# Rotary queries and keys projected channels-first, with partner channels fetched by transfers within SBUF

## The chip, the cores and the metric

One core of one Trainium2 chip runs the whole program in one launch. The metric is the device time in microseconds. Its median over three runs of the kernel before is 974.03 us (973.75 to 974.24).

## What is computed

A decoder trunk of two layers over 256 tokens of 1024 channels, float32. Each layer is a SwiGLU block, a hybrid mixer and a second SwiGLU block, each followed by a layer norm. The change touches the mixer alone, and in it the eight rotary heads (group C):

```python
def rope(t, positions):                      # HEAD_DIM = 64
    ang = positions[:, None] * inv[None, :]  # 32 frequencies
    ang = concatenate([ang, ang], axis=-1)
    t1, t2 = split(t, 2, axis=-1)
    return t * cos(ang) + concatenate([-t2, t1], axis=-1) * sin(ang)

def hybrid_mixer(x, ...):
    proj = x @ w_in
    a_val, a_gate, bq, bk, bv, bf, cq, ck, cv = split(proj, ...)
    y_a = conv_module(a_val, a_gate, ...)            # 256 channels, causal, 31 taps
    y_b = forgetting_attention(bq, bk, bv, bf, ...)  # 4 heads of 64, no rotary
    qc = rope(heads(cq, 8), positions) * (64 ** -0.5)
    kc = rope(heads(ck, 8), positions)
    y_c = dilated_attention(qc, kc, cv)              # 8 heads of 64
    return concatenate([y_a, y_b, y_c]) @ w_o
```

Queries and keys are 512 columns each of `x @ w_in`. The partner of channel c of a head is channel c + 32 or c - 32 of the same head.

## The kernel before

All work is ordered by hand: five engine programs (SyncE, TensorE, ScalarE, VectorE, GpSimd), each run in its written order, tied by counting semaphores. TensorE is called PE, ScalarE ACT, VectorE DVE below, as in the profile.

Weights arrive in units of 128 x 2048 values (1 MB) in a ring of three slots. For each unit ACT rounds the raw values to `w_hi` (`split_hi`, L888), DVE forms the rest `w_lo` (`split_lo`, L1113), and PE uses three products per piece, hi x hi, hi x lo and lo x hi. A slot's next `split_hi` waits until PE has used the slot (`unit_used`), and its next load until `split_lo` is done (`lo_done`). The mixer's units are 0 and 1 (convolution input), 2 and 3 (rotary queries), 4 and 5 (rotary keys), 6 (values and forget gates of group B), 7 and 8 (values of group C), 9 and 10 (queries and keys of group B), 11 to 14 (output projection).

Two forms of projection exist. `project` (L463 to L481) holds 128 tokens of the input as PE's stationary operand and streams 512 weight columns past it: 12 matmuls of 512 columns for a unit and a tile of tokens, 24 for a unit; the result has tokens on the partitions. `project_T` (L741 to L756) holds 128 weight columns and streams the 256 tokens: 48 matmuls of 256 columns for a unit; the result has channels on the partitions. Before the change only units 9 and 10 use `project_T`.

The order of the mixer around the change (`mixer` of each engine: PE L802, ACT L995, DVE L1361):

- PE: units 2 and 3 into `ybank[0:2]`, with the transposes of the convolution's input (`conv_input_T`) between them; units 4 and 5 into `ybank[2:4]`; `rotated_T` for n = 0, 1 (four 128 x 128 transposes each, through L426); unit 6 into `bank[0:2]`; unit 7; `rotated_T` for n = 2, 3; unit 8; then eight steps of attention. A step takes the scores of a pair of heads (L670), the transposes of the previous pair's probabilities (`probs_T`, L426), the products with the values of that pair (`values`, L737), and between these the pieces of units 9 to 14 that `FILL` lists.
- DVE: `split_lo` of units 5 to 10, and between them the rotation `rope(l, n)` (L1251 to L1270; n = 0, 1 queries and n = 2, 3 keys of token tile n % 2), which reads the projection in PSUM, twice multiplies and once adds 128 x 512 values; `gate_sums` behind `split_lo(8)`; `log_gates` behind `split_lo(9)`; and the 31 taps of the convolution (`taps`, L1283, two instructions a tap) in the gaps: 5 taps after `gate_sums`, 4 after `log_gates`, the last in step 5. In a step DVE masks the scores and takes their maximum (`mask_and_max`, L1338), and normalises the probabilities (`inverse`, `normalise`).
- ACT: `split_hi` of units 5 to 10, and between them `rotated_out(n)` (L1014 to L1019), which copies the transposed queries and keys out of PSUM into `qT` and `kT`, the values' copies (L1027, L1041) and the gates' exponential and logarithm. In a step it copies the transposed probabilities of the previous pair's first head (`probs_out`, L1044), takes the exponentials of this pair's two heads (`exponent`, L1050), and only then copies those of the previous pair's second head.
- PE's waits in the steps that matter here: `values` waits for both heads' transposed probabilities (L724), the transposes of the convolution's result (`conv_out_T`, L697 to L703) for the last tap.

Of the kernel before, what the change touches and what calls it, by code (L numbers as in the profile page):

```python
# [20 lines left out]
ALU = mybir.AluOpType  # L21
# [3 lines left out]
P = 128  # L25
SEQ, D, DEPTH = 256, 1024, 2
T = SEQ // P
KT = D // P
# [77 lines left out]
def consts_array():  # L106
# [4 lines left out]
    cos = np.cos(ang).astype(np.float32).reshape(T, P, 32).transpose(1, 0, 2).reshape(P, -1)  # L111
    sin = np.sin(ang).astype(np.float32)
    sgn = np.concatenate([-sin, sin], axis=1).reshape(T, P, 64).transpose(1, 0, 2).reshape(P, -1)
# [15 lines left out]
def trunk(nc, x, w_in, w_o, ffn_in, ffn_out, ln_gb, conv_wb, rows, consts, out):  # L129
    with ExitStack() as ctx:  # L130
        def sb(name, shape, dt=F32):
            return ctx.enter_context(nc.sbuf_tensor(name, shape, dt))
# [35 lines left out]
        rope_c = sb("rope_c", [P, DIL_H * HD])  # L168
        rope_s = sb("rope_s", [P, DIL_H * HD])
        qk = sb("qk", [P, 2, DIL_H * HD])  # L170
# [21 lines left out]
        for width in (P, 2 * P, 2 * CAUSAL, T * 32, T * 64):  # L192
# [3 lines left out]
        cos_t = cos_t.rearrange("p (t e) -> p t e", t=T)  # L196
        sin_t = sin_t.rearrange("p (t e) -> p t e", t=T)
# [44 lines left out]
        rope_mul = counted("rope_mul", 2 * T)  # L242
        rope_ready = counted("rope_ready", 2 * T)
# [12 lines left out]
        qk_psum = counted("qk_psum", 2 * T)  # L256
        qkT_ready = counted("qkT_ready", 2 * T + 2)
# [155 lines left out]
        def _(eng):  # L413
# [236 lines left out]
            def scores(l, s):  # L650
# [13 lines left out]
                eng.wait_ge(qkT_ready, count(qkT_ready, l, 2 * T + 2 * fox))  # L664
# [22 lines left out]
            def gate_sums_T(l):  # L687


                eng.wait_ge(lf_ready, count(lf_ready, l, 2))  # L690
                eng.wait_ge(qkT_ready, count(qkT_ready, l, 2 * T))
# [20 lines left out]
            def probs_T(l, p, i):  # L712

                h = 2 * p + i
                eng.wait_ge(p_ready, count(p_ready, l, h + 1))
                if h > 0:

                    eng.wait_ge(pT_ready, count(pT_ready, l, h))
                transposes(bank[2], [prob[:, h % 4, j * P:(j + 1) * P] for j in range(3)]).then_inc(pT_psum, 1)
# [21 lines left out]
            def project_T(slot, half, m, last_unit=None):  # L741
# [4 lines left out]
                dst, cols = ybank[m // 2][:, (m % 2) * SEQ:(m % 2 + 1) * SEQ], slice(m * P, (m + 1) * P)  # L746
# [43 lines left out]
            def rotated_T(l, which, last_unit):  # L790

                for n in which:

                    eng.wait_ge(rope_ready, count(rope_ready, l, n + 1))
                    if n == 1:
                        eng.wait_ge(uT_ready, count(uT_ready, l, 1))
                    if n >= 2:
                        eng.wait_ge(qkT_ready, count(qkT_ready, l, n - 1))
                    transposes(bank[3 - n % T], [qk[:, n % T, p * P:(p + 1) * P] for p in range(4)],
                               last_unit if n % T == 0 else None).then_inc(qk_psum, 1)  # L800

            def mixer(l):  # L802
# [15 lines left out]
                def halves(u, dst, last_unit=None, between=None, at=None):  # L818

                    for half in range(2):  # L820
                        wait_unit(l, b + u + half)
                        for t in range(T):
                            m = project(dst[t][:, :], (u + half) % RING, half, t,
                                        last_unit=last_unit if half == t == 0 else None)
# [4 lines left out]
                            if half == 0 and t == at:  # L829
                                between()  # L830
# [6 lines left out]
                halves(2, ybank[0:2], unit_used, conv_input_T, 0)  # L837
                halves(4, ybank[2:4], unit_used)
                rotated_T(l, range(2), unit_used)

                wait_unit(l, b + 6)
                for t in range(T):
                    project(bank[t][:, 0:FVF], 6 % RING, 0, t, FVF, KT).then_inc(proj_done, 1)
# [36 lines left out]
        def _(eng):  # L880
# [26 lines left out]
            def begin_sum(l, j, t):  # L907

                if j == 1 and t == 0:
                    eng.wait_ge(qkT_ready, count(qkT_ready, l, 2 * T + 2))  # L910
# [84 lines left out]
            def mixer(l):  # L995
# [4 lines left out]
                for t in range(T):  # L1000
# [13 lines left out]
                def rotated_out(n):  # L1014
                    t = n % T
                    eng.wait_ge(qk_psum, count(qk_psum, l, n + 1))
                    dst = (qT, kT)[n // T]
                    eng.activation(dst[:, :, t * P:(t + 1) * P], bank[3 - t][:, :].rearrange("p (k n) -> p k n", k=4),
                                   ACT.Copy, scale=-HD ** -0.5 if n < T else 1.0).then_inc(qkT_ready, 1)  # L1019

                rotated_out(0)
                rotated_out(1)
# [11 lines left out]
                rotated_out(2)  # L1034
                rotated_out(3)
# [18 lines left out]
                for s in range(STEPS):  # L1054
# [13 lines left out]
                    for i in range(2 if s == FQ_STEP else 0):  # L1068
# [3 lines left out]
                                       ACT.Copy, scale=(-HD ** -0.5, 1.0)[i]).then_inc(qkT_ready, 1)  # L1072
# [33 lines left out]
        def _(eng):  # L1106
# [144 lines left out]
            def rope(l, n):  # L1251

                t, src = n % T, ybank[n]
                eng.wait_ge(proj_done, count(proj_done, l, T + n + 1))
                if n > 0:

                    eng.wait_ge(rope_ready, count(rope_ready, l, n))
                eng.tensor_tensor(rope_c[:, :].rearrange("p (g e) -> p g e", e=32),
                                  src[:, :].rearrange("p (g e) -> p g e", e=32),
                                  cos_t[:, t:t + 1, :].broadcast_to([P, 2 * DIL_H, 32]), ALU.mult)  # L1260
                halves = dict(h=DIL_H, s=2)
                swapped = src[:, :].rearrange("p (h s e) -> p h s e", **halves)[:, :, ::-1, :]
                sin4 = sin_t[:, t, :].rearrange("p (h s e) -> p h s e", h=1, s=2).broadcast_to([P, DIL_H, 2, 32])
                eng.tensor_tensor(rope_s[:, :].rearrange("p (h s e) -> p h s e", **halves), swapped, sin4, ALU.mult)\
                   .then_inc(rope_mul, 1)
                if n >= T:

                    eng.wait_ge(qk_psum, count(qk_psum, l, n - T + 1))
                eng.wait_ge(rope_mul, count(rope_mul, l, n + 1))
                eng.tensor_tensor(qk[:, n % T, :], rope_c[:, :], rope_s[:, :], ALU.add).then_inc(rope_ready, 1)  # L1270
# [90 lines left out]
            def mixer(l):  # L1361
# [139 lines left out]
```

## Time and profile before

| | |
|---|---|
| median of three runs | 974.03 us |
| the profiled execution | 973.58 us |
| its span, first to last instruction | 971.8 us |
| PE, DVE, ACT busy | 959.7, 654.5, 503.1 us |
| mixer of layer 0, from its first projection to the second block's | about 201 to 308 us of the span |
| mixer of layer 1 | about 680 to 787 us |

The profile is one execution on the chip. A timeline gives for each instruction its start and its length; neighbours on one engine overlap a little in it, since an instruction's tail is counted in its length, so the pace of a queue is read from the starts. An entry in brackets is the idle time ahead of an instruction and what ended it. The chain of work that ended last is followed back from the last instruction. The two mixers run alike, 478.57 us apart, so the first stands for both.

### The profile page before, as it was taken

What the parts mean: (1) busy time and instruction counts of PE and PEld (TensorE: products, weight loads), DVE (VectorE), ACT (ScalarE), POOL (GpSimd) and SP (SyncE); (2) the same over time, 40 slices, a digit from 0 to 9 for tenths busy, and PEclk for the clock granted to TensorE, in tenths of its full rate; (3) what the DMA queues carried; (4) which work ended last, traced back from release to release, by engine and by line L of the source; (5) the groups of instructions that cost most, each with busy time, mean ns of one, the idle gap of its engine ahead of it and who ended that gap; (6) DMA issues with size and microseconds to landing.
All of it is one profiled execution on the core that took longest, in us unless ns stands there. A gap on an engine that the chain in (4) does not pass through costs nothing.

```text
span 971.8 us, 14695 instructions
## 1 busy us (share of the span) xinstructions
PE 959.7 (99%) x5263; PEld 814.8 (84%) x5263; DVE 654.5 (67%) x950; ACT 503.1 (52%) x672; POOL 29.1 (3%) x27
## 2 busy tenths in 40 slices
PE   8999999999999999999999999999999999999997
PEld 6988888888878988888888888888888788888885
DVE  6555656689998565655675565657999875565565
ACT  6454455445774445545454455544457654554541
POOL 0000000010001000000010000002000010000000
PEclk9999999999999999999999999999999999999999
DMA  9656566565325656557555656565643355655551
GB/s 313 235 173 216 173 202 227 188 217 174 131 88 162 228 173 200 188 182 245 166 186 174 215 174 196 193 219 183 233 162 115 120 194 175 194 195 176 197 189 43
DMA packets 123586, 180.05 MB, mean 185 GB/s; under 512 B 5792, under 2 KB 98080, under 8 KB 122784
## 3 DMA queue, kind: packets, MB, share of 16 engines
q1 hardware_dynamic: 123264, 178.91, 55.6%
q0 software_dynamic: 144, 0.62, 0.2%
q8 instruction: 22, 0.36, 0.1%
q14 instruction: 12, 0.10, 0.0%
q10 hardware_dynamic: 144, 0.07, 0.0%
HBM read 178.52 MB, written 1.05 MB: 185 GB/s over the span
## 4 chain that ended last, share of the span: by engine, by line
PE 98%; DVE 1%; ACT 0%; issue 0%; DVEq 0%
PE bank L549 27%; PE bank L551 14%; PE ybank L500 10%; PE ybank L506 10%; PE ybank L504 10%; PE bank L426 3%; PE bank L472 2%; PE bank L479 2%; PE bank L476 2%; PE ybank L472 2%; PE ybank L479 2%; PE ybank L476 2%; PE bank L533 2%; PE bank L529 2%; PE bank L535 2%; PE bank L670 1%
## 5 line engine op out<-in xcount | busy, mean ns | idle before, releaser
L1113 DVE TENSOR_TENSOR w_lo<-raw,w_hi 128x2048 fp32r<-128x2048 f32 (+1 forms) x155 | 355.2, 2292 | 241.5 <-ACT w_hi L888 241.5
L888 ACT ACTIVATE w_hi<-raw 128x2048 fp32r<-128x2048 f32 x160 | 305.8, 1911 | 254.7 <-PE ybank L506 112.8
L549 PE MATMUL bank<-xT,w_hi 128*128 128x512 f32 x1152 | 401.0, 392 | 0.0
L551 PE MATMUL bank<-xT,w_lo 128*128 128x256 f32 x1152 | 323.7, 281 | 0.0
L549 PEld LDWEIGHTS bank<-xT,w_hi 128*128 128x128 f32 x1152 | 216.3, 188 | 47.3
L551 PEld LDWEIGHTS bank<-xT,w_lo 128*128 128x128 f32 x1152 | 216.7, 188 | 1.5
L500 PE MATMUL ybank<-w_hi,yT_hi 128*128 128x512 f32 x416 | 165.9, 399 | 0.3
L506 PE MATMUL ybank<-w_hi,yT_lo 128*128 128x512 f32 x416 | 162.9, 392 | 0.0
L504 PE MATMUL ybank<-w_lo,yT_hi 128*128 128x512 f32 x416 | 161.9, 389 | 0.0
L500 PEld LDWEIGHTS ybank<-w_hi,yT_hi 128*128 128x128 f32 x416 | 78.2, 188 | 18.0 <-issue 2.6
L506 PEld LDWEIGHTS ybank<-w_hi,yT_lo 128*128 128x128 f32 x416 | 77.8, 187 | 18.4
L504 PEld LDWEIGHTS ybank<-w_lo,yT_hi 128*128 128x128 f32 x416 | 78.2, 188 | 14.4
L937 ACT ACTIVATE gate<-gate 128x256 f32<-128x256 f32 x72 | 30.1, 418 | 48.4 <-DVE gate L1194 48.4
L930 ACT ACTIVATE gate<-bank 128x256 f32<-128x256 f32 x72 | 27.7, 385 | 51.1 <-PE bank L551 51.1
L1283 DVE SCALAR_TENSOR_TENSOR acc<-uT,cwb,acc 128x256 f32<-128x256 f32 x120 | 50.2, 479 | 0.1
L472 PE MATMUL bank<-w_hi,xT 128*128 128x512 f32 (+1 forms) x112 | 41.5, 370 | 1.3 <-ACT xT L903 1.3
L1194 DVE TENSOR_TENSOR gate<-bank,gate 128x256 f32<-128x256 f32 x72 | 30.3, 421 | 16.8 <-ACT gate L930 16.8
L476 PE MATMUL bank<-w_lo,xT 128*128 128x512 f32 (+1 forms) x112 | 40.4, 361 | 0.0
L1201 DVE TENSOR_TENSOR hid<-gate,hid 128x256 f32<-128x256 f32 x72 | 30.6, 426 | 11.5 <-ACT gate L937 11.5
L472 PE MATMUL ybank<-w_hi,xT 128*128 128x512 f32 x96 | 38.2, 398 | 0.0
L479 PE MATMUL ybank<-w_hi,xT 128*128 128x512 f32 x96 | 37.7, 393 | 0.0
L476 PE MATMUL ybank<-w_lo,xT 128*128 128x512 f32 x96 | 37.6, 392 | 0.0
(133 smaller groups left out, 986.6 us busy)
## 6 DMA issues: line engine op xcount, KB each, us to landing
raw<-in_ffn_in SPq DMA_DIRECT2D x172, 512.0 KB, 4.6
raw<-in_ffn_out SPq DMA_DIRECT2D x88, 512.0 KB, 3.9
raw<-in_w_in SPq DMA_DIRECT2D x40, 512.0 KB, 4.5
raw<-in_w_o SPq DMA_DIRECT2D x16, 512.0 KB, 3.6
gb<-in_ln_gb SPq DMA_DIRECT2D x6, 1024.0 KB, 7.2
raw<-in_w_in SPq DMA_DIRECT2D x4, 520.0 KB, 6.2
raw<-in_ffn_in SPq DMA_DIRECT2D x8, 256.0 KB, 5.4
xn<-in_x SPq DMA_DIRECT2D x4, 256.0 KB, 4.3
```

Source lines behind the costliest of these rows:

```text
L472: m = eng.matmul(dst, xT_hi[:, kk, tok], wh[:, k, :], start=kk == 0 and not onto, stop=False, skip_group_check=onto)
L476: m = eng.matmul(dst, xT_hi[:, kk, tok], wl[:, k, :], start=False, stop=False, skip_group_check=onto)
L479: m = eng.matmul(dst, xT_lo[:, kk, tok], wh[:, k, :], start=False, stop=kk == KT - 1, skip_group_check=onto)
L500: m = eng.matmul(dst, aT_hi[:, k, tok], wh[:, k, cols], start=False, stop=False, skip_group_check=True)
L504: eng.matmul(dst, aT_hi[:, k, tok], wl[:, k, cols], start=False, stop=False, skip_group_check=True)
L506: m = eng.matmul(dst, aT_lo[:, k, tok], wh[:, k, cols], start=False, stop=ends is not None and k == 1, skip_group_check=True)
L549: eng.matmul(dst[:, :], wh[:, k, g, cols], xT[:, kk, :, :].rearrange("p a n -> p (a n)"), start=kk == 0, stop=False, skip_group_check=True)
L551: m = eng.matmul(dst[:, SEQ:2 * SEQ], wl[:, k, g, cols], xT_hi[:, kk, :], start=False, stop=kk == KT - 1, skip_group_check=True)
L888: eng.activation(w_hi[:, s, 0:width], raw[:, s, 0:width], ACT.Copy).then_inc(hi_done, 1)
L1113: eng.tensor_tensor(w_lo[:, s, 0:width], raw[:, s, 0:width], w_hi[:, s, 0:width].bitcast(F32), ALU.subtract).then_inc(lo_done, 1)
L1201: eng.tensor_tensor(hid[:, j, :], gate[:, j, :], hid[:, j, :], ALU.mult).then_inc(h_ready, 1)
L1283: eng.scalar_tensor_tensor(acc[:, cb, :], src, w, acc[:, cb, :], ALU.mult, ALU.add)\
```

## The change

Units 2 to 5 are projected by `project_T`, so the queries and keys leave PE with channels on the partitions, two heads to a bank half. ACT copies them from PSUM to `qk_raw` (two copies of 128 x 512 for the queries, two for the keys) and scales the queries there. Four transfers of 32 partitions x 4 KB each, issued from ACT's queue behind the copies, write every 32-channel half to the place of its partner in `qk_swap`. DVE multiplies `qk_raw` by the cosines into `qT` or `kT` (`rope_cos`), multiplies `qk_swap` by the signed sines once the transfers have landed, and adds (`rope_sin`); each is one instruction of 128 x 1024 values. PE's sixteen transposes a layer (`rotated_T`) and ACT's four copies behind them (`rotated_out`) are gone. The tables of cosines and sines grow from 192 to 512 columns of the constants.

```diff
@@ PE
+                def halves_T(u, first_bank, between=None):
+                    for half in range(2):
+                        wait_unit(l, b + u + half)
+                        for m in range(4):
+                            e = project_T((u + half) % RING, half, m, unit_used if half == m == 0 else None, first_bank)
+                            if half == 1 and m % 2 == 1:
+                                e.then_inc(proj_done, 1)
...
-                halves(2, ybank[0:2], unit_used, conv_input_T, 0)
-                halves(4, ybank[2:4], unit_used)
-                rotated_T(l, range(2), unit_used)
+                halves_T(2, 0, conv_input_T)
+                halves_T(4, 2)
...
-                eng.wait_ge(rope_mul, count(rope_mul, l, 2 * T))
-                halves(7, ybank[2:4], unit_used, lambda: rotated_T(l, range(2, 4), None), 1)
+                eng.wait_ge(qk_copied, count(qk_copied, l, 4))
+                halves(7, ybank[2:4])
@@ ACT
+                def rotary_out(n):
+                    for i in range(2):
+                        eng.wait_ge(proj_done, count(proj_done, l, T * (n + 1) + i + 1))
+                        eng.activation(qk_raw[:, n, 2 * i:2 * i + 2, :],
+                                       ybank[2 * n + i][:, :].rearrange("p (k n) -> p k n", k=2), ACT.Copy,
+                                       scale=(-HD ** -0.5, 1.0)[n]).then_inc(qk_copied, 1)
+                    eng.wait_ge(qk_copied, count(qk_copied, l, 2 * n + 2))
+                    for g in range(4):
+                        to, of = 32 * g, 32 * (g + 1 - 2 * (g % 2))
+                        eng.dma_start(qk_swap[to:to + 32, n, :, :], qk_raw[of:of + 32, n, :, :])\
+                           .then_inc(swap_loaded[n], 16)
                 split_hi(l, b, 5)
+                rotary_out(0)
                 split_hi(l, b, 6)
                 split_hi(l, b, 7)
...
-                rotated_out(0)
-                rotated_out(1)
+                rotary_out(1)
                 split_hi(l, b, 8)
...
-                rotated_out(2)
-                rotated_out(3)
                 split_hi(l, b, 10)
@@ DVE
+            def rope_cos(l, n):
+                eng.wait_ge(qk_copied, count(qk_copied, l, 2 * n + 2))
+                eng.tensor_tensor((qT, kT)[n][:, :, :], qk_raw[:, n, :, :],
+                                  cos_t.broadcast_to([P, DIL_H // 2, SEQ]), ALU.mult).then_inc(rope_mul, 1)
+            def rope_sin(l, n):
+                eng.wait_ge(swap_loaded[n], count(swap_loaded[n], l, 64))
+                eng.tensor_tensor(qk_swap[:, n, :, :], qk_swap[:, n, :, :],
+                                  sin_t.broadcast_to([P, DIL_H // 2, SEQ]), ALU.mult).then_inc(rope_mul, 1)
+                eng.wait_ge(rope_mul, count(rope_mul, l, 2 * n + 2))
+                eng.tensor_tensor((qT, kT)[n][:, :, :], (qT, kT)[n][:, :, :], qk_swap[:, n, :, :], ALU.add)\
+                   .then_inc(rope_ready, 1)
...
                 split_lo(l, b, 5)
-                rope(l, 0)
+                rope_cos(l, 0)
                 split_lo(l, b, 6)
-                rope(l, 1)
                 taps(l, TAPS_AT["unit", 6])
                 split_lo(l, b, 7)
-                rope(l, 2)
-                rope(l, 3)
+                rope_sin(l, 0)
+                rope_cos(l, 1)
                 split_lo(l, b, 8)
                 gate_sums(l)
+                rope_sin(l, 1)
                 taps(l, TAPS_AT["unit", 8])
                 split_lo(l, b, 9)
```

The semaphores follow: the scores wait for `rope_ready` where they waited for `qkT_ready`, `project_T` takes the number of its first bank, and the release of unit 5's slot moves to the first matmul of unit 6.

## Rows read from the trace of the kernel before

**Rows 1.** The page's busy times and the chain that ended last.

```profile
PE 959.7 (99%) x5263; PEld 814.8 (84%) x5263; DVE 654.5 (67%) x950; ACT 503.1 (52%) x672; POOL 29.1 (3%) x27
PE 98%; DVE 1%; ACT 0%; issue 0%; DVEq 0%
```

**Rows 2.** Chain that ended last, layer 0 (start us, length us, what): the removed transposes.

```profile
229.54 0.87 PE bank L426 x8
...
241.68 0.87 PE bank L426 x8
```

**Rows 3.** Timeline of PE, 512 columns (start, length, engine, line, operation, operands, count).

```profile
210.21 0.39 PE L476 MATMUL ybank<-w_lo,xT 128*128 128x512 f32 x1
...
229.15 0.39 PE L479 MATMUL ybank<-w_hi,xT 128*128 128x512 f32 x1
```

**Rows 4.** Timeline of PE, 256 columns, piece (9, 0, 1) to (9, 1, 1).

```profile
251.24 0.28 PE L753 MATMUL ybank<-xT,w_hi 128*128 128x256 f32 x1
...
255.29 0.28 PE L754 MATMUL ybank<-xT,w_lo 128*128 128x256 f32 x1
```

**Rows 5.** Timeline of ACT around units 7 to 9.

```profile
224.05 1.92 ACT L888 ACTIVATE w_hi<-raw 128x2048 fp32r<-128x2048 f32 x1 [3.31 <-PE ybank L479]
230.02 1.09 ACT L1018 ACTIVATE qT<-bank 128x512 f32<-128x512 f32 x2 [4.05 <-PE bank L426]
230.99 1.92 ACT L888 ACTIVATE w_hi<-raw 128x2048 fp32r<-128x2048 f32 x1
...
236.21 0.39 ACT L1027 ACTIVATE fv<-bank 128x256 f32<-128x256 f32 x1 [2.49 <-PE bank L479]
```

**Rows 6.** Timeline of DVE from unit 8's `split_lo` to step 1's mask.

```profile
233.70 2.28 DVE L1113 TENSOR_TENSOR w_lo<-raw,w_hi 128x2048 fp32r<-128x2048 f32 x1
235.90 0.15 DVE L1313 TENSOR_TENSOR fz<-bank,small 128x4 f32<-128x4 f32 x1
236.63 0.16 DVE L1313 TENSOR_TENSOR fz<-bank,small 128x4 f32<-128x4 f32 x1 [0.57 <-ACT fv L1027]
...
236.91 4.04 DVE L1283 SCALAR_TENSOR_TENSOR acc<-uT,cwb,acc 128x256 f32<-128x256 f32 x10
...
249.03 0.29 DVE L1338 CUSTOM_DVE_ANT_0 masked<-bank,cst 128x128 f32<-128x128 f32 x1 [0.35 <-PE bank L670]
...
256.45 0.29 DVE L1338 CUSTOM_DVE_ANT_0 masked<-bank,cst 128x128 f32<-128x128 f32 x1 [0.97 <-PE bank L670]
...
257.01 0.08 DVE L1338 DVE_READ_ACCUMULATOR2_ANT negmax<- 128x1 f32 x1
```

**Rows 7.** DVE groups by shape: count, then busy us and mean ns of one.

```profile
L1144 DVE TENSOR_TENSOR w_lo<-raw,w_hi 128x1024 fp32r<-128x1024 f32 x5 | 6.1, 1219 | 0.0
L1270 DVE TENSOR_TENSOR qk<-rope_c,rope_s 128x512 f32<-128x512 f32 x8 | 5.5, 693 | 0.6
```

**Rows 8.** DMA issues: ACT's only one, in its timeline; then SP's of L358 (ns min/median/max) and their landing.

```profile
0.75 0.41 ACTq L1096 DMA_DIRECT2D cst<-in_consts  x1
...
L358 SPq DMA_DIRECT2D raw<-in_w_in x44: 367/418/615, 171.3 to 708.7; - x44
...
DMA to landing us min/median/max: 3.1/4.1/6.8
```

**Rows 9.** Timeline of all engines in step 1: exponential, second copy, products with the values.

```profile
257.32 0.39 ACT L1050 ACTIVATE prob<-masked,negmax 128x128 f32<-128x128 f32 x1
...
259.08 0.48 ACT L1044 ACTIVATE probT<-bank 128x384 f32<-128x384 f32 x1
...
260.00 0.63 PEld L737 LDWEIGHTS bank<-probT,cv 128*64 128x64 f32 x8
```

**Rows 10.** Timeline of all engines where the convolution's last tap meets PE.

```profile
284.49 0.87 DVE L1283 SCALAR_TENSOR_TENSOR acc<-uT,cwb,acc 128x256 f32<-128x256 f32 x2
...
284.89 0.49 PE L426 MATMUL bank<-cst,prob 128*128 128x128 f32 x3
...
285.51 0.63 PE L426 MATMUL bank<-cst,acc 128*128 128x128 f32 x4
```

More of the change, by code:

```diff
@@ L191, in trunk @@
         at, view = 0, []
-        for width in (P, 2 * P, 2 * CAUSAL, T * 32, T * 64):
+        for width in (P, 2 * P, 2 * CAUSAL, SEQ, SEQ):
             view.append(cst[:, at:at + width])
@@ L241, in trunk @@
         u_ready = counted("u_ready", T)
-        rope_mul = counted("rope_mul", 2 * T)
-        rope_ready = counted("rope_ready", 2 * T)
+        qk_copied = counted("qk_copied", 4)
+        swap_loaded = [counted(f"swap_loaded{n}", 4 * 16) for n in range(2)]
+        rope_mul = counted("rope_mul", 4)
+        rope_ready = counted("rope_ready", 2)
         cv_ready = counted("cv_ready", T)
@@ L662, in scores @@
                 qs, ks = (fqT, fkT) if fox else (qT, kT)
-                eng.wait_ge(qkT_ready, count(qkT_ready, l, 2 * T + 2 * fox))
+                if fox:
+                    eng.wait_ge(fqkT_ready, count(fqkT_ready, l, 2))
+                else:
+                    eng.wait_ge(rope_ready, count(rope_ready, l, 2))
                 for t, (cols, keys) in enumerate(((slice(0, P), P), (slice(P, CAUSAL), SEQ))):
@@ L718, in probs_T @@
                     eng.wait_ge(pT_ready, count(pT_ready, l, h))
+                else:
+                    eng.wait_ge(uT_ready, count(uT_ready, l, 1))
                 transposes(bank[2], [prob[:, h % 4, j * P:(j + 1) * P] for j in range(3)]).then_inc(pT_psum, 1)
@@ L739, in values, with project_T @@
                 m.then_inc(pv_done, 1)
-            def project_T(slot, half, m, last_unit=None):
+            def project_T(slot, half, m, last_unit=None, first_bank=0):
                 wh = w_hi[:, slot, 0:UNIT].rearrange("p (k n) -> p k n", k=4)
                 wl = w_lo[:, slot, 0:UNIT].rearrange("p (k n) -> p k n", k=4)
-                dst, cols = ybank[m // 2][:, (m % 2) * SEQ:(m % 2 + 1) * SEQ], slice(m * P, (m + 1) * P)
+                dst = ybank[first_bank + m // 2][:, (m % 2) * SEQ:(m % 2 + 1) * SEQ]
+                cols = slice(m * P, (m + 1) * P)
                 for k in range(4):
@@ L788, in fill @@
                         m.then_inc(unit_used, 1)
[L790 to L800, printed above, removed]
             def mixer(l):
@@ L816, in mixer, with halves @@
                     project(bank[t][:, :], 1, 1, t).then_inc(proj_done, 1)
-                def halves(u, dst, last_unit=None, between=None, at=None):
+                def halves(u, dst):
                     for half in range(2):
@@ L823, in halves @@
                             m = project(dst[t][:, :], (u + half) % RING, half, t,
-                                        last_unit=last_unit if half == t == 0 else None)
+                                        last_unit=unit_used if half == t == 0 else None)
                             if half == 1:
@@ L828, in halves @@
                                 m.then_inc(unit_used, 1)
-                            if half == 0 and t == at:
+                def halves_T(u, first_bank, between=None):
[5 more added lines that the diff above has]
+                                e.then_inc(proj_done, 1)
+                            if half == 0 and m == 3:
+                                e.then_inc(unit_used, 1)
+                            if half == 0 and m == 1 and between is not None:
                                 between()
@@ L909, in begin_sum @@
                 if j == 1 and t == 0:
[L910 removed]
+                    eng.wait_ge(fqkT_ready, count(fqkT_ready, l, 2))
                 elif j == 1:
```

47 lines of the change are left out of this document (11 added, 36 removed).

## The prediction, made before the changed kernel was run

> **What bounds the kernel now.** I read the page first: PE is busy 99% of the span and makes 98% of the chain that ended last [rows 1]. So a microsecond of PE work removed is worth a microsecond, unless PE then meets a wait that its own work covers today. Both mixers must therefore be read queue by queue, to see how far behind PE the other two engines are where PE waits for them. Two places matter. In step 1 PE loads the first values' weights at 260.00, while the copy that it needs begins at 259.08 and ends at 259.56 [rows 9]: ACT is 0.44 us ahead of PE, no more. At the end of the convolution DVE's last tap ends at 284.49 + 0.87 = 285.36, PE's preceding transposes end at 285.38, and the transposes of the taps' result follow at 285.51 [rows 10]: DVE and PE arrive together. A faster PE alone gains nothing beyond these two meetings. The question is what the change does to DVE and ACT.
>
> **PE: what goes and what comes.** Two blocks of eight transposes leave the chain, 0.87 us each [rows 2], 1.74 us a layer. In their place 96 matmuls of 512 columns become 192 of 256. The columns streamed are the same; the pace is not. From the start at 210.21 to that at 229.15 lie 82 matmuls of 512: 0.2310 us each [rows 3]. From 251.24 to 255.29 lie 34 of 256: 0.1191 us each [rows 4]. So 192 x 0.1191 - 96 x 0.2310 = 22.87 - 22.18 = 0.69 us more. PE alone would be 1.74 - 0.69 = 1.05 us a layer ahead at the end of unit 8, 2.1 us in all. These prices come from this trace in the same form and the same bank pattern, so I give them 0.1 us a layer of doubt.
>
> **ACT: four copies stay four copies, eight issues are new.** Of the copies only the place changes: the old ones read 128 x 512 from PSUM as the new ones do. New is that ACT issues four transfers behind each pair. The only issue of ACT in the trace takes 0.41 us; SP's take 0.37 to 0.62, median 0.42 [rows 8]. I take 0.42, so 1.68 us for four; the bounds are 0 (the queue hands them over and goes on) and 0.62. The first four push units 6's `split_hi` from 218.8 to about 221.2 and its `split_lo` to about 225.4; PE wants unit 6 at about 230.1, so this is covered. The second four are not covered. PE ends unit 5 at 229.38 + 0.69 = 230.07, with its tail 230.25. ACT's last copy ends at 230.85, the issues at 232.6, and `split_hi(8)` runs from 232.6 to 234.5, where it began at 230.99 [rows 5]. PE itself wants unit 8 only at about 241.4, so the wait behind is DVE's.
>
> **DVE: the same work, placed later.** Twelve instructions of 128 x 512 (0.69 us) become six of 128 x 1024, 1.22 us by the row of that shape [rows 7]. That is 8.3 against 7.3 us, a small gain, but in the wrong place: before, all four rotations are done when `split_lo(8)` begins at 233.70. After, that `split_lo` waits for ACT until 234.5, ends its slot at 236.7, the two small sums and the minimum follow to about 237.05, and then `rope_sin` of the keys stands in the queue: 1.22 + 0.03 + 1.14 = 2.4 us (the trace shows about 0.08 us of overlap between neighbours and none across a wait on one's own result). The five taps that began at 236.91 [rows 6] begin at about 239.45. DVE is 2.54 us late from there. Nothing in its queue is shorter up to step 1; what absorbs the delay is its waiting for PE today: 0.35 us ahead of step 0's mask, 0.97 us ahead of step 1's [rows 6] and 0.08 us ahead of the first reciprocal (a gap between starts). That makes 1.40, and leaves step 1's masks 2.54 - 1.40 = 1.14 us late. The price of a 1024-value instruction is bounded below by 0.69 (the 512-value row) and above by 1.22; I take the row of its shape.
>
> **The waits that the change adds, and who stands behind them.** `rope_cos` of the keys waits for ACT's copy at 230.85 and starts no earlier than DVE's `rope_sin` of the queries lets it, at about 232.3; behind it stands only `split_lo(8)`, which waits longer for ACT. PE's wait for `qk_copied` ahead of unit 7 (235.9) is met five microseconds earlier. `rope_sin` of the keys waits for the last transfer, issued at about 232.2. Transfers of L358 land 3.1 to 6.8 us after their issue, median 4.1, at four times the size of one of these [rows 8]; nothing in the trace moves data within SBUF. At 4.1 the last lands at 236.3, 0.75 us ahead of need. I take it as on time; the far bound is 6.8, landing at 239.0, 1.95 us late. Behind that wait stand all of DVE's queue up to the masks. The larger table of constants adds 160 KB to one load at the start, under weight loads that PE does not wait for in that stretch; I price it at 0, at most 0.5 us.
>
> **Where the queues meet again.** In step 1 the exponentials wait for the masks. The first starts at 257.32 today, with its maximum ready at 257.01 + 0.09 = 257.10 [rows 6, 9]. It moves to 257.10 + 1.14 + 0.04 = 258.28, 0.96 us later, and the copy behind the two exponentials ends at 260.52 instead of 259.56. PE's first products with values then start at about 260.56, where they start at 260.00 today. PE reaches that point 1.05 us earlier than now, at 258.95, and waits 1.6 us. So the gain of 1.05 us a layer turns into a loss of 0.56. From there on ACT and DVE wait for PE again and again, and the last tap meets PE as before, so I carry the shift unchanged to the layer's end. The sum is 2 x 0.56 = 1.1 us: from the profiled execution's 973.58 to 974.7, and from the median of the runs, which is 0.45 us higher, to 975.1 us.
>
> **Rivals.** A: the transfers land late. The loads of the next unit are in flight at the same time: unit 7's `split_lo` frees a slot at about 230, and its 1 MB fills the DMA engines until about 234. If the last transfer takes the 6.8 us of the slowest load, DVE loses 1.95 us more a layer, undiminished, since its idle time is used up: 2 x (0.56 + 1.95) = 5.0, and 979.0 us. It decides from a landing 4.8 us after the last issue. This is the case on the slow side. The Trainium skill, "SBUF — State Buffer", section "Door 1: The DMA port swizzle", holds that a transfer on 32 partitions reaches only 8 of 16 ports, and that two such transfers serialize; its 218 GB/s for 8 ports makes 2.4 us of the 512 KB, and with its fixed 2 us an estimate of 4.4 us from the first issue, before any share taken by the load. No row here shows a transfer on 32 partitions.
>
> B: ACT's issues cost nearly nothing. Then `split_hi(8)` begins at about 231.0, DVE's next bound is the values' copy at 236.4 [rows 5], and the taps begin at 239.1: 0.35 us less, 0.2 us a layer, 974.5 us. For it speaks nothing in the rows, whose every issue holds its queue for 0.37 us or more. The Trainium skill, "DMA: Bandwidth & Descriptors", section "Anatomy of one DMA", gives about 50 ns of sequencer time to a dispatch (on another path), which would be this case.
>
> C: part of PE's gain lands. It needs both ends at once, cheap issues as in B and DVE's 1024-value instructions at the 0.69 us of the 512-value row. Then the keys' sine pair takes 1.4 us, the taps begin at 238.1, DVE reaches step 1's mask 1.20 - 0.43 = 0.77 us later than the 255.48 at which it is free today, so 0.2 us earlier than it masks now, and the products with the values can start at 259.4 instead of 260.00: 0.6 us a layer gained, 972.8 us. All of PE's 1.05 us, 971.9 us, would need DVE earlier still by half a microsecond. Against it speaks the row of the shape.
>
> The change does what it says in each of these: no transposes of queries and keys remain, whoever wins.
>
> **How the numbers follow.** The forecast has 0.5, from 974.3 to 976.2 (0.3 us a layer for DVE's price and the small gaps, 0.62 for 0.42 in the issues above). A has 0.2, spread from 976.2 to 979 by the landing. B has 0.18. C has 0.12, of which a third lies under 972.1. A measurement of this kernel tells about 0.2%, 1.95 us, from no change: below 972.1 is faster, above 976.0 is slower. Faster gets that third of C and a little for the doubt, 0.06; slower gets A and 0.07 from the forecast's upper edge and from waits that I haven't seen, 0.27; the rest, 0.67, is the same. The range goes from 971.9, all of C, to 978.5, most of A.
>
> **What would show each step.** PE's starts in units 2 to 5 should lie 0.119 us apart, units 2 to 5 together should take 0.7 us longer than now, and unit 8 about 1.05 us earlier. ACT's queue should show four issues of about 0.42 us behind the keys' copies, and `split_hi(8)` about 1.6 us later than now. DVE's 1024-value instructions should take 1.22 us, its five taps begin 2.5 us later, and the waits ahead of the masks of steps 0 and 1 should be gone. PE should wait about 1.6 us ahead of L737 in step 1 of each layer, for ACT, and nowhere else for more than 0.3 us. DVE waiting for the transfers ahead of the keys' sine product shows A; ACT's queue going straight on, B; no PE wait at L737, C. A PE wait for a weight unit, or a DVE instruction of 1024 values far from 1.22 us, would make the working wrong, not only its result.

## The result, and the profile after

The changed kernel takes 979.72 us, median of 6 runs (978.88 to 981.45), where the kernel before takes 974.00 beside it (973.71 to 974.78): 1.006 times as long, 95% interval 1.005 to 1.007. It is slower by 5.7 us, and the forecast of 975.1 with its range up to 978.5 was wrong. The profiled execution took 979.14 us.

To compare stages I measure from one instruction to the same one later: VectorE's (DVE's) doubled `xT<-bank` at the mixer's start and again at the start of the SwiGLU block behind it. The first pair is from DVE's timeline of the kernel before, the second from that of the changed kernel (start, length, what, and in brackets the idle time before it and who ended it):

```profile
201.11 1.29 DVE L1131 TENSOR_TENSOR xT<-bank,xT 128x512 fp32r<-128x512 f32 x2 [1.01 <-ACT xT L903]
308.19 1.29 DVE L1131 TENSOR_TENSOR xT<-bank,xT 128x512 fp32r<-128x512 f32 x2 [1.02 <-ACT xT L903]
```

```profile
201.63 1.29 DVE L1138 TENSOR_TENSOR xT<-bank,xT 128x512 fp32r<-128x512 f32 x2 [1.02 <-ACT xT L907]
311.12 1.29 DVE L1138 TENSOR_TENSOR xT<-bank,xT 128x512 fp32r<-128x512 f32 x2 [1.01 <-ACT xT L907]
```

The mixer's 107.08 us became 109.49, and the second layer's, read the same way, went from 107.08 to 109.59. That is 2.41 + 2.51 = 4.9 us. The other 0.52 us of the profiled span lie ahead of the first mixer, whose start varies from 200.8 to 202.4 us in the traces of the runs below with no order by their edits, so I don't count them as an effect of the change. Positions below are counted from the mixer's start: 35.80, say, is 236.91 less 201.11.

The page of the changed kernel, which answers to [rows 1]:

```profile
PE 958.5 (98%) x5423; PEld 821.0 (84%) x5423; DVE 652.6 (67%) x938; ACT 503.8 (52%) x672; POOL 29.2 (3%) x27
PE 91%; DVE 5%; DMA 2%; ACT 1%; issue 0%; ACTq 0%; SPq 0%; DVEq 0%
```

DVE's share of the chain that ended last grew from 1% to 5%, and DMA (the transfers) appears in it with 2%. That chain in layer 0 shows why (start, length, what):

```profile
230.78 0.61 ACT qk_raw L1018
231.41 0.51 ACTq L1024
...
231.96 0.61 ACTq L1024
...
232.60 0.62 ACTq L1024
...
233.24 6.27 DMA qk_swap<-qk_raw
239.53 1.24 DVE qk_swap L1267
240.79 1.23 DVE kT L1270
242.02 3.96 DVE acc L1284 x10
...
259.92 0.29 DVE masked L1339
...
260.59 0.59 ACT prob L1057 x3
...
262.46 0.38 ACT probT L1051
...
262.88 0.87 PE bank L742 x8
```

From the copy of the keys at 230.78 to the first values at 262.88 the chain runs outside TensorE (PE): ScalarE's (ACT's) issues, one transfer, all of DVE's queue up to step 1's masks, and the softmax. In ACT's timeline the four issues and what stands behind them, which answers to [rows 5], where `split_hi(8)` began at 230.99:

```profile
220.01 2.75 ACTq L1024 DMA_DIRECT2D qk_swap<-qk_raw  x4
222.87 1.94 ACT L892 ACTIVATE w_hi<-raw 128x2080 fp32r<-128x2080 f32 x1 [2.89 <-issue]
...
231.41 2.45 ACTq L1024 DMA_DIRECT2D qk_swap<-qk_raw  x4
233.96 1.92 ACT L892 ACTIVATE w_hi<-raw 128x2048 fp32r<-128x2048 f32 x1 [2.58 <-issue]
```

DVE's timeline, which answers to [rows 6, 7]. The taps of unit 8 begin at 40.31 instead of 35.80, and step 1's masks at 58.29 instead of 55.34, with no wait ahead of them any more:

```profile
235.91 2.29 DVE L1120 TENSOR_TENSOR w_lo<-raw,w_hi 128x2048 fp32r<-128x2048 f32 x1 [0.63 <-ACT w_hi L892]
...
239.53 1.23 DVE L1267 TENSOR_TENSOR qk_swap<-qk_swap,cst 128x1024 f32<-128x1024 f32 x1 [0.99 <-DMA qk_swap<-qk_raw]
...
241.94 4.04 DVE L1284 SCALAR_TENSOR_TENSOR acc<-uT,cwb,acc 128x256 f32<-128x256 f32 x10
...
259.92 0.29 DVE L1339 CUSTOM_DVE_ANT_0 masked<-bank,cst 128x128 f32<-128x128 f32 x1
```

PE's waits over both layers (us in total, times, longest). The first is at step 1's products with values, 2.2 us a layer, and the other two are at the transposes of the probabilities. None of them stood in the kernel before:

```profile
PE bank L742 <- ACT probT L1051: 4.4, 2, 2.2
...
PE bank L427 <- DVE prob L1350: 1.0, 2, 0.5
PE bank L427 <- ACT probT L1051: 0.9, 2, 0.4
```

That is 6.3 us of waiting, 3.15 a layer. It eats the 1.05 us a layer by which PE's work shrank, and the 2.1 us left make most of the 2.4 us that the mixer grew by. The rest is gaps of 0.3 us or less behind other short waits.

### The profile page after: what moved, and what is told of

Same layout as the page of the kernel before. It is cut to its first block, busy times and chain, and to the rows that moved or that the text cites. A ratio compares the mean times of both kernels' runs of the same rounds, so it can differ in the third digit from the quotient of the medians.

```text
span 977.2 us, 15003 instructions
## 1 busy us (share of the span) xinstructions
PE 958.5 (98%) x5423; PEld 821.0 (84%) x5423; DVE 652.6 (67%) x938; ACT 503.8 (52%) x672; POOL 29.2 (3%) x27
## 3 DMA queue, kind: packets, MB, share of 16 engines
HBM read 178.69 MB, written 1.05 MB: 184 GB/s over the span
## 4 chain that ended last, share of the span: by engine, by line
PE 91%; DVE 5%; DMA 2%; ACT 1%; issue 0%; ACTq 0%; SPq 0%; DVEq 0%
PE bank L550 27%; PE bank L552 14%; PE ybank L501 10%; PE ybank L507 10%; PE ybank L505 10%; DVE acc L1284 2%; PE bank L473 2%; PE bank L427 2%; PE bank L480 2%; PE bank L477 2%; PE ybank L760 2%; PE ybank L755 2%; PE ybank L759 2%; PE bank L534 2%; PE bank L530 2%; PE bank L536 2%
## 5 line engine op out<-in xcount | busy, mean ns | idle before, releaser
L755 PE MATMUL ybank<-xT,w_hi 128*128 128x256 f32 x192 | 55.3, 288 | 0.0
L760 PE MATMUL ybank<-xT,w_lo 128*128 128x256 f32 x192 | 54.1, 282 | 0.0
L759 PE MATMUL ybank<-xT,w_hi 128*128 128x256 f32 x192 | 54.1, 282 | 0.0
```

The lines of the kernel that those rows point to most:

```text
L755: e = eng.matmul(dst, wh[:, k, cols], xT_hi[:, kk, :], start=kk == 0 and m % 2 == 0, stop=False, skip_group_check=True)
L759: eng.matmul(dst, wh[:, k, cols], xT_lo[:, kk, :], start=False, stop=False, skip_group_check=True)
L760: e = eng.matmul(dst, wl[:, k, cols], xT_hi[:, kk, :], start=False, stop=kk == KT - 1, skip_group_check=True)
```

## The experiments

The column of step 1's masks has their start in us from the mixer's start, in layer 0. A star marks a mixer in which the granted clock fell (see e9 to e11).

| kernel | median us | ratio to before (95%) | step 1's masks | mixers, layer 0 and 1 |
|---|---|---|---|---|
| before | 974.0 | | 55.34 | 107.08, 107.08 |
| changed | 979.72 | 1.006 (1.005 to 1.007) | 58.29 | 109.49, 109.59 |
| e1 nobody waits for the transfers | 978.25 | 1.0046 (1.0029 to 1.0063) | 57.20 | 108.40, 109.68* |
| e2 no transfers | 974.09 | 1.0001 (0.9992 to 1.0011) | 56.00 | 107.22, 107.22 |
| e3 one wide transfer each | 974.24 | 1.0002 (0.9992 to 1.0011) | 56.00 | 107.21, 107.22 |
| e4 fewer transposes in before | 971.83 | 0.9979 (0.997 to 0.9989) | 54.43 | 106.16, 106.16 |
| e5 issues on SyncE | 974.15 | 1.0004 (0.9994 to 1.0013) | 56.00 | 107.23, 107.19 |
| e6 e5, and taps moved | 971.52 | 0.9978 (0.9969 to 0.9988) | 54.41 | 106.08, 106.00 |
| e7 taps moved alone | 974.90 | 1.001 (1.0001 to 1.0019) | 56.40 | 107.69, 107.56 |
| e8 projections alone in before | 975.34 | 1.0013 (1.0004 to 1.0023) | 56.01 | 107.74, 107.82 |
| e9 unit 10's load held back | 978.72 | 1.0047 (1.003 to 1.0064) | 57.20 | 109.70*, 109.70* |
| e10 keys' transfers alone | 979.79 | 1.0058 (1.0041 to 1.0075) | 57.28 | 110.09*, 109.93* |
| e11 transfers of 2 KB | 979.15 | 1.0055 (1.0038 to 1.0072) | 57.24 | 109.95*, 109.97* |

**e1: the sine product does not wait for the transfers.**

```diff
-                eng.wait_ge(swap_loaded[n], count(swap_loaded[n], l, 64))
-                eng.tensor_tensor(qk_swap[:, n, :, :], qk_swap[:, n, :, :], ...
+                eng.tensor_tensor(sine[:, :, :], qk_raw[:, n, :, :], ...
```

> The changed kernel with its transfers issued as before, but the sine product reads the untouched channels (qk_raw) into a tile of its own, so nothing waits for a landing; the partner exchange is thus left out of the result. Theory 1 (four issues of 0.61 us each on ACT hold up split_hi(8), and DVE then waits 1.0 us more for the landing): the issue part stays, the landing part goes, so each layer is about 1.0 us shorter than in the changed kernel: the five taps begin 1.0 us earlier, and the total is about 977.5 us (changed kernel 979.7). Theory 2 (the landing alone is what costs, issues are cheap): most of the 5.7 us goes, about 974.5. Theory 3 (the transfers' traffic slows the weight loads, or the 256-column products are dearer than counted): nothing changes, 979.5.

Layer 0's mixer took 108.40 us, 1.09 less than with the wait, and step 1's masks came 1.09 us earlier: that is what waiting for the landing costs. The second layer's 109.68, and with it the total above the 977.5 expected, is explained under e9. 1.3 us of loss remain without any such wait, so the landing alone is not the story.

**e2: e1 without the issues and the transfers** (the four `dma_start` and the wait ahead of them removed).

> As e1, and the eight transfers of a layer are not issued at all. Theory 1: split_hi(8) begins right behind the keys' second copy, 2.5 us earlier than in the changed kernel; DVE's next bound is the values' copy; a layer is 0.2 us longer than before the change, and the total about 974.5 us. Theory 3: still near 979. A rival on the other side: PE's lead of 1.05 us a layer lands in full, 971.9.

974.09 us, and 107.22 a mixer: the issues cost 108.40 - 107.22 = 1.18 us a layer. The remaining 0.14 is what all other edits cost together, PE's saving of 1.05 us included: PE still waits 1.1 us for step 1's values.

**e3: one transfer of all 128 partitions in place of four of 32.** The bytes and the place in ACT's queue are the same.

```diff
-                    for g in range(4):
-                        to, of = 32 * g, 32 * (g + 1 - 2 * (g % 2))
-                        eng.dma_start(qk_swap[to:to + 32, n, :, :], qk_raw[of:of + 32, n, :, :])\
-                           .then_inc(swap_loaded[n], 16)
+                    eng.dma_start(qk_swap[:, n, :, :], qk_raw[:, n, :, :]).then_inc(swap_loaded[n], 16)
```

> The changed kernel with one transfer of 128 partitions (512 KB, same bytes) instead of four of 32 for the queries, and one for the keys; each channel lands in its own place, so the partner exchange is left out of the result. Theory 1, issue cost goes by the number of transfers: ACT's issue takes 0.6 us instead of 2.45, the landing is waited for no longer (issued 1.9 us earlier relative to need), total 974.5 to 975.5. If the issue cost goes by the partitions or bytes moved: the one issue takes 2 us or more and the total stays at 978 or above. If narrow transfers land late because they reach few ports, the landing after the last issue falls from 6.3 us to under 4.5 us; if not, it stays at 5 to 6 us.

974.24 us. The transfers of this kernel, by tile: their issues' ns (min/median/max), and their landing:

```profile
L1022 ACTq DMA_DIRECT2D qk_swap<-qk_raw x4: 472/472/530, 220.7 to 710.8; - x4
...
DMA to landing us min/median/max: 4.4/5.4/6.8
```

These figures are over both layers and over queries and keys. The keys' transfer of layer 0, in a view of 231 to 240 us:

```profile
qk_swap<-qk_raw ACTq DMA_DIRECT2D x1, 512.0 KB, 4.4
```

It lands 4.4 us after its issue (4.8 in layer 1), where the last of the keys' four narrow ones took 6.3 and 6.4 in the changed kernel. DVE does not wait for it, and it takes both gains to get there: the one issue starts 1.84 us before the fourth of four, and it lands 1.9 us faster. With 6.3 us it would land at 29.77 + 6.3 = 36.1, and the sine product starts at 35.62. It has unit 10's load ahead of it, issued at 27.98, instead of beside it. So e3 alone does not tell whether the width or the load made the landing shorter (e9 does). The same 512 KB in one issue costs 0.5 us of ACT where four cost 2.45.

**e4: is a faster PE worth anything?** Two of four transposes are left out of each block in the kernel before; half of the rotated channels are not transposed.

```diff
-                    transposes(bank[3 - n % T], [qk[:, n % T, p * P:(p + 1) * P] for p in range(4)],
+                    transposes(bank[3 - n % T], [qk[:, n % T, p * P:(p + 1) * P] for p in range(2)],
```

> The kernel before the change with two of the four transposes in each block of rotated_T left out (eight of sixteen a layer; half of the rotary channels are thus wrong). PE has 0.87 us a layer less work and ACT and DVE are unchanged. Theory of the prediction (DVE and PE arrive together at the last tap, so a faster PE alone gains nothing): the kernel stays within 0.5 us of 974.0. Rival (DVE's meeting with PE moves along, because DVE waits for PE several times in the steps before): the gain lands, 2 x 0.87 = 1.7 us, 972.3.

971.83 us, 0.92 us less a mixer: all of PE's saving arrived. At the place where the prediction let DVE's last tap meet PE, which answers to [rows 10], all engines' timeline of e4 reads:

```profile
283.76 0.87 DVE L1283 SCALAR_TENSOR_TENSOR acc<-uT,cwb,acc 128x256 f32<-128x256 f32 x2
284.16 0.49 PE L426 MATMUL bank<-cst,prob 128*128 128x128 f32 x3
...
284.78 0.63 PE L426 MATMUL bank<-cst,acc 128*128 128x128 f32 x4
```

DVE's last tap moved from 83.38 to 82.47 after the mixer's start, with PE. DVE waits for PE ahead of the masks (0.98 us ahead of step 1's, as before), so it follows a faster PE. The meeting is no limit to the 0.9 us tried here.

**e5: the same eight transfers issued by SyncE (SP)**, the queries' behind unit 8's loads, the keys' behind unit 9's. It computes all that the changed kernel does.

```diff
                         load_unit(l, u, view, w_l[:, 4 * half:4 * half + 4, col:col + BANK])
+                        if u in (8, 9):
+                            swap(u - 8)
```

> The changed kernel with the eight transfers of a layer issued from SP's queue (the queries' behind the load of unit 8, the keys' behind that of unit 9) instead of ACT's; the result is complete. Theory 1 (ACT's time for the issues is the larger part of the loss): split_hi(8) follows the keys' second copy at once, the transfers land before DVE comes to them or at most 0.5 us late, the mixer takes 107.2 to 107.6 us (before 107.08, changed 109.49), the total is 974.4 to 975.0. Rival: on SP the issues stand ahead of weight loads and delay these; then ACT waits for a load ahead of a split_hi and the total stays above 977.

974.15 us, like e2. The keys' issues took SP 2.42 us, where nothing waits for it. Unit 10's load stands behind them in SP's queue, they landed in 2.2 to 2.4 us, and DVE did not wait for them.

**e6: e5 with taps moved** into DVE's idle time, their order unchanged.

```diff
                 split_lo(l, b, 5)
+                taps(l, range(6, 7))
                 rope_cos(l, 0)
                 split_lo(l, b, 6)
-                taps(l, TAPS_AT["unit", 6])
+                taps(l, range(7, 10))
...
                 split_lo(l, b, 8)
+                taps(l, range(10, 11))
                 gate_sums(l)
+                taps(l, range(11, 14))
                 rope_sin(l, 1)
-                taps(l, TAPS_AT["unit", 8])
```

> e5 with three of the convolution's taps moved into DVE's idle time: one ahead of the queries' cosine product, one behind split_lo(8) ahead of the gate sums, and the last one that moves counts against the five taps behind the gate sums, of which three are left, ahead of the keys' sine product. Theory (PE's 1.05 us a layer is real and is lost only to DVE's lateness at step 1): DVE reaches the masks of step 1 before PE's scores are there, PE has no wait at L737, the mixer takes 106.0 to 106.3 us, and the total is 971.9, 2.1 us under the kernel before. Rival (the last tap meets PE without slack, so that DVE's total work sets the end of the mixer): total 973 to 974.

971.52 us (11 runs, 971.26 to 972.58), faster than both kernels, and it too computes all that the changed kernel does. The mixer takes 106.08 and 106.00 us, 1.0 and 1.08 less than before. In its timeline the copy is done ahead of PE again, as in [rows 9], and the values start at 57.84 where they started at 58.89. The order of the taps alone was not tried in the kernel before; there PE has no wait in the mixer that earlier taps could shorten (it is busy for 106.57 of the 107.08 us). The lines of e6:

```profile
257.99 0.48 ACT L1054 ACTIVATE probT<-bank 128x384 f32<-128x384 f32 x1
258.92 0.63 PEld L750 LDWEIGHTS bank<-probT,cv 128*64 128x64 f32 x8
```

**e7: the same order of taps, issues left on ACT.**

> The changed kernel with only the order of the taps of e6; the transfers stay on ACT's queue. Theory 1: ACT's 2.45 us stay ahead of split_hi(8), but DVE has 1.6 us less between the gate sums and step 1, and the keys' sine product stands 2.4 us behind the gate sums, so that nothing waits for the landing any more. DVE is late by about 2 us less: the mixer takes 107.6 to 108.0 us, total 975.3 to 976. If only DVE's order mattered and not ACT's issues, it would come to e6's 971.9.

974.90 us, 0.4 below what was expected. With other work between, DVE no longer waits for the transfers, but the issues still make it late: PE waits 1.5 us for the values.

**e8: only units 2 to 5 projected channels-first** in the kernel before, by matmuls of 256 columns; what is read from the banks afterwards is then not queries and keys.

> The kernel before the change with units 2 to 5 projected channels-first and nothing else changed: the rotation then works on the wrong layout, so the rotary heads are wrong; it prices the 192 matmuls of 256 columns alone. By the paces of the trace a layer is 0.69 us longer, total 975.4. By N/2.4 us plus a fixed part for each matmul it would be 0.25 us a layer, 974.5. If more is hidden in it (weights in another place, banks), more than 976.

975.34 us. The mixers grew by 0.66 and 0.74 us, where the prediction had 0.69.

**e9: unit 10's load held back until the keys' transfers have landed.** What makes a landing take 6.3 us? SP issues unit 10's 1 MB in two halves, first in the kernel before, then in the changed one:

```profile
229.69 0.88 SPq L358 DMA_DIRECT2D raw<-in_w_in  x2
```

```profile
231.84 0.89 SPq L359 DMA_DIRECT2D raw<-in_w_in  x2
```

That is 28.58 and 30.21 after the mixer's start, and 231.84 lies between the first and the second of the keys' issues.

```diff
+                        if u == 10:
+                            wait_apart(swap_loaded[1], count(swap_loaded[1], l, 64))
                         load_unit(l, u, view, w_l[:, 4 * half:4 * half + 4, col:col + BANK])
```

> The changed kernel, whose loads of unit 10 wait on SyncE's queue until the keys' four transfers have landed. Theory: those four took 6.3 us because unit 10's 1 MB, pushed back by 2 us through ScalarE's first four issues, starts at the same moment (231.84 against 231.41). Then, with the load behind them, the last lands in 2.2 to 3.5 us, VectorE no longer waits 0.99 us for it, the mixer takes 108.4 us instead of 109.5 and the kernel 977.6 us. Rival: four transfers of 32 partitions are that slow by themselves: the landing stays above 5 us, and the kernel takes 979.7 us or, where unit 10 now comes late for TensorE, more.

The landings of the keys' four transfers of layer 0 by themselves, first in the changed kernel, then in e9 (from the view of `qk_swap` in 230 to 236 us):

```profile
DMA to landing us min/median/max: 2.4/5.7/6.3
```

```profile
DMA to landing us min/median/max: 2.2/2.3/2.4
```

In layer 1 they are 2.4/5.7/6.4 and again 2.2/2.3/2.4. In the changed kernel it is the first of the four, issued ahead of the load, that takes 2.4 us; the three behind the load's issue take 5.1 to 6.3. So the load makes them late, and not their 32 partitions, which e9 left as they were. The rival is out. DVE starts the sine product without a wait:

```profile
236.06 2.29 DVE L1122 TENSOR_TENSOR w_lo<-raw,w_hi 128x2048 fp32r<-128x2048 f32 x1 [0.64 <-ACT w_hi L894]
...
238.61 1.22 DVE L1269 TENSOR_TENSOR qk_swap<-qk_swap,cst 128x1024 f32<-128x1024 f32 x1
```

Step 1's masks come at 57.20, as in e1. Yet the mixers take 109.70, not the 108.4 expected. The cause is in the granted clock behind PE's wait. Stretches of 3.4 us, from the first values on, in e9 from the clock's fall 0.9 us behind them (stretch, its length, busy us and instructions of PE, PEld, DVE, ACT and POOL, then granted clock, DMA share, GB/s), first e9, then e1 in its two layers, then the changed kernel in its two:

```profile
262.90:266.30 3.40, 3.40 (x18) 2.75 (x19) 3.06 (x15) 1.46 (x6) 0.00 (x0) 0.50 0.80 305
```

```profile
262.20:265.60 3.40, 3.40 (x31) 2.75 (x32) 3.33 (x17) 2.46 (x7) 0.00 (x0) 1.00 0.49 176
742.20:745.60 3.40, 3.40 (x20) 2.28 (x21) 2.68 (x15) 1.22 (x3) 0.00 (x0) 0.55 0.57 192
```

```profile
262.90:266.30 3.40, 3.40 (x31) 2.75 (x32) 3.33 (x17) 2.46 (x7) 0.00 (x0) 1.00 0.51 160
744.00:747.40 3.40, 3.40 (x31) 2.75 (x32) 3.33 (x17) 2.46 (x7) 0.00 (x0) 1.00 0.57 194
```

After a wait of 2.2 us PE was granted 1.2 GHz instead of 2.4 for some 3.4 us in e9: 18 matmuls passed where 31 do at full clock. That cost 109.70 - 108.40 = 1.3 us, against e1's layer 0 with its masks at the same 57.20. In e1 it happened in one layer of two, at the same wait, and in the profiled execution of the changed kernel in neither.

**e10: the changed kernel without the queries' transfers** (`for g in range(4 * n)`; the queries' sine product reads their own channels).

> The changed kernel without the queries' four transfers; their sine product reads the queries' own channels, so the queries' partner exchange is left out. Theory: ScalarE's first four issues are what pushes unit 10's loads onto the keys' transfers. Without them split_hi(6) starts on time, the loads are issued about 27.9 us after the mixer's start, ahead of the keys' transfers at 29.8, as in the kernel with one transfer each, and VectorE does not wait for the keys' transfers; the four keys' issues stay, so the mixer takes 108.0 to 108.5 us and the kernel 976.9 to 977.8. Rival: the late landing is the keys' own: VectorE waits as before for them, 109.5 us and 979.7.

Unit 10's load is issued at 27.82, ahead of the keys' transfers again; these land in 3.5/3.7/3.9 us, and DVE does not wait for them. So it was the queries' four issues that put the load onto the keys' transfers. The time missed its expectation for the reason found in e9: PE waited 2.2 us and the clock fell to 0.50 for 3.4 us in both layers.

**e11: e1 with transfers of 2 KB** (32 partitions of 16 elements).

> The kernel whose transfers nobody reads (e1), with each transfer cut from 128 KB to 2 KB (32 partitions of 16 elements); the partner exchange is left out as there. If an issue's price goes by their number, the eight issues still take 0.51 to 0.62 us each and the kernel what e1 took, 977.3 to 978.6, with both mixers at about 108.4. Rival: the issue's price goes by bytes or packets, then each takes 0.45 us or less and the kernel 976 or less. If e1's second mixer (109.68 us) was long through traffic, both are 108.4 here.

The issues of this kernel:

```profile
L1025 ACTq DMA_DIRECT2D qk_swap<-qk_raw x16: 542/610/613, 219.1 to 713.9; - x16
```

Their price did not move although the bytes fell to a 64th: between these two sizes it goes by the number of transfers. The time, 979.15, again missed its expectation of up to 978.6: the clock fell in both layers behind the same wait of 2.2 us. So the transfers' own traffic is not what makes it fall.

## Why the prediction was wrong

**The mechanism was right, and so was its place.** PE's lead of 1.05 us is real (e6's mixers are 1.0 and 1.08 shorter; e8 confirms the 0.69), it was lost at step 1's values, and it was DVE's lateness that took it. The 1024-value instructions took 1.22 us, as priced. ACT's second copy of the keys began 29.15 us behind the mixer's start, where I had 29.14. DVE's idle time absorbed 4.51 - 2.95 = 1.56 us, where I had 1.40. How lateness turns into time was right too. In the mixers without a star where PE waits at the values, the mixer's growth is the masks' lateness less about 0.5: 2.95 gave 2.41, 1.86 gave 1.32 (e1), 1.06 gave 0.61 (e7), 0.66 gave 0.14 (e2). My 1.14 for 0.56 lies on that line. So the error is all ahead of the taps: 4.51 us of lateness, not 2.54. Of the 1.97 us between them the four issues make 0.77 (2.45 against 1.68) and DVE's wait for the landing 0.99; the rest is gaps of about 0.1.

**First step that failed: the size of an issue.** "I take 0.42, so 1.68 us for four." They took 2.45, 0.61 to 0.62 each behind the first, which was the far bound I had given (0.62). `split_hi(8)` began at 32.33, where I had 31.5. The 0.42 is from SP's loads of [rows 8], which it issues two at a time; I had no row for four in a row, and still took the median instead of the bound. What stood with rival B, the Trainium skill's "DMA: Bandwidth & Descriptors", section "Anatomy of one DMA", with some 50 ns a dispatch on another path, does not hold for these queues: no issue of the mixers' transfers took ACT or SP less than 0.33 us in the changed kernel.

**Second step that failed: the landing, "I take it as on time".** It rested on 4.1 us behind the last issue; it took 6.27, and DVE waited 0.99 us. What I had missed stands in "so this is covered". I followed the queries' four issues to PE's need of unit 6, and there they were covered. I did not follow them to SP. They made `split_hi(6)` late (the wait of 2.89 us above), DVE's `split_lo` of units 6 and 7 behind it, and with that the slot that SP fills with unit 10. The load moved from 28.58 to 30.21, into the keys' transfers. Without the queries' issues it is at 27.82 (e10). Held behind the keys' transfers (e9: 2.2 to 2.4 us) or ahead of them (e10: 3.5 to 3.9) it no longer makes DVE wait. Rival A had the loads as its reason, but put their slot at about 230, from the kernel before, and not where the change moves it.

**Third: the far bounds were taken one at a time.** A's 979.0 us is close to the profiled 979.14, but by other terms: it had 6.8 us of landing behind issues of 0.42. The issues at 0.61 and the landing at 6.27 came together, since the first causes part of the second. e1 and e2 give them 1.09 + 1.18 = 2.27 of the 2.41 us.

Of A's page, the Trainium skill's "SBUF — State Buffer", section "Door 1: The DMA port swizzle", the runs give no test. My estimate by it, 4.4 us from the first issue to the last landing, is close to e9's 4.2 with the load out of the way; but 1.8 of these are ACT's issuing, and each transfer landed in 2.2 to 2.4. One transfer of 128 partitions landed in 4.4 to 6.8 us, always beside a load. Other lengths or an idle memory weren't tried.

**Fourth: the meeting at the last tap.** That "a faster PE alone gains nothing beyond these two meetings" was wrong (e4, e6): two engines that end together need not be independent, and here the one follows the other. It changed nothing in this forecast, which never got that far.

**Not foreseen: the clock.** 974.0 + 4.9 makes 978.9. The two executions of the changed kernel with a mean granted clock of 0.999 took 978.88 and 979.14; the other four, at 0.995 to 0.997, took 979.65 to 981.45. Where I have traces of such a deficit (e1, e9 to e11), it lies behind the 2.2 us wait; for these four it is inferred, since only their mean clock is known. It would explain the 0.6 to 0.8 us by which the median is above the two. It does not carry the miss: the two executions without it are still above my range.

## What to carry to other kernels

Price every new DMA issue on a compute engine by the number of transfers (here 0.6 us each in a row) and put them on a queue that nobody waits behind; the same eight transfers cost 2.3 us a layer on ScalarE (1.2 for the issues, 1.1 for the late landing) and nothing that I could measure on SyncE. Follow a late instruction through everything that it releases, down to the loads of the units behind, because a load that moves can collide with another transfer. A saving on the bounding engine appears only when the engines that feed it are made early enough as well: with the issues moved and some taps brought forward, the same change went from 5.7 us slower to 2.3 us faster.

## What the runs showed of the hardware

- An issue's time does not depend on its bytes: 0.54 to 0.61 us for 2 KB, 0.51 to 0.62 for nearly all of 128 KB on 32 partitions, and 0.47 to 0.53 for 512 KB on 128 partitions, the only ones that stood alone. Whether it is the standing alone or the 128 partitions that makes the last cheaper wasn't separated.
- Transfers of 128 KB within SBUF, four issued 0.6 us apart, landed in 2.2 to 2.4 us each with a 1 MB load held back behind them (e9, e5), in 3.5 to 3.9 with it issued some 2 us ahead (e10), and in 5.1 to 6.4 where it was issued among them, all but the first, which took 2.4 (changed kernel).
- After waits of 2.2 us PE's granted clock fell to 0.5 for about 3.4 us in seven of ten mixers that show such a wait (changed kernel, e1, e9 to e11). The fall began 0.0 to 0.9 us behind the wait's end, and the mixer took 1.3 to 1.6 us more than the masks' lateness gives by the line above. After waits of 1.1 to 1.5 us (e2, e3, e5, e7) it fell in none of eight. What decides between falling and not at the same wait stays open. A wait that is just too long can thus cost more than its length.
